# Router logits with stationary weights in four column groups, and the output norm's factors multiplied into the output weights

## The reference, cut to what matters

```python
o = jnp.concatenate([rms_norm(oa, p['out_norm_a']), rms_norm(ob, p['out_norm_b'])], axis=-1)
x = x + jnp.einsum('bse,ed->bsd', o, p['w_o'])
h2 = rms_norm(x, p['norm_ffn'])
x = x + expert_choice_moe(h2, p['w_router'], p['w_gate'], p['w_up'], p['w_down'])
...
logits = jnp.einsum('nd,de->ne', xf, w_router).astype(jnp.float32)
aff = jax.nn.softmax(logits, axis=-1)
gates, idx = lax.top_k(aff.T, cap)
```

## Time and profile before

| | |
|---|---|
| median of 3 runs | 1052.97 us (1052.86 to 1053.31) |
| the profiled execution | 1052.84 us |
| its span from the first to the last instruction | 1051.1 us |
| PE / DVE / ACT / POOL busy | 1015.7 / 897.5 / 780.7 / 504.9 us |
| mean granted TensorE clock | 0.992 |

### The profile page before, as it was taken

How to read it: one execution, slowest core, us unless ns; L and a number is a source line. 1 busy time by engine, 2 the same in 40 slices (tenths; PEclk the granted TensorE clock), 3 DMA queues, 4 the chain that set the end, 5 groups by cost and what they waited for, 6 DMA issues and landing times.

```text
span 1051.1 us, 16370 instructions
## 1 busy us (share of the span) xinstructions
PE 1015.7 (97%) x5361; PEld 865.1 (82%) x5361; DVE 897.5 (85%) x1128; ACT 780.7 (74%) x1071; POOL 504.9 (48%) x458
## 2 busy tenths in 40 slices
PE   8999999999999999995999999999999999999997
PEld 7999977888788888884888888888888888888885
DVE  6788779999988954478999999999999999999982
ACT  7665569999999844446778877788778877788772
POOL 2477689555599764544532444234432444234001
PEclk9999999999999999997999999999999999999999
DMA  9345150211332278753899999999999999999982
GB/s 324 80 127 121 69 203 16 47 32 41 111 95 78 85 212 261 207 171 121 346 377 398 405 413 401 401 398 420 399 403 399 400 418 401 402 397 415 408 343 40
DMA packets 83359, 272.90 MB, mean 260 GB/s; under 512 B 32929, under 2 KB 41340, under 8 KB 59500
## 3 DMA queue, kind: packets, MB, share of 16 engines
q1 hardware_dynamic: 77504, 254.96, 64.2%
q0 software_dynamic: 5744, 17.29, 6.6%
q10 hardware_dynamic: 60, 0.01, 0.0%
HBM read 245.89 MB, written 26.35 MB: 259 GB/s over the span
## 4 chain that ended last, share of the span: by engine, by line
PE 50%; DMA 1%; DVE 1%; issue 0%; ACT 0%; POOLq 0%; POOL 0%
PE ps L2166 11%; PE ps L2168 11%; PE ps L2167 11%; PE ps L2182 5%; PE ps L2181 5%; PE ps L2180 5%; PE ps L2133 1%; DMA out<-y,give 1%; DMA xt<-h,idxT 0%; DVE idx L1914 0%; DVE affT L1923 0%; DVE gates L1909 0%; POOLq L2440 0%; POOL out L2125 0%; ACT y L2294 0%
## 5 line engine op out<-in xcount | busy, mean ns | idle before, releaser
L2336 DVE TENSOR_TENSOR lo<-raw,hi 128x2048 fp32r<-128x2048 f32 x191 | 430.7, 2286 | 29.5 <-ACT hi L2258 29.3
L2258 ACT ACTIVATE hi<-raw 128x2048 fp32r<-128x2048 f32 x192 | 364.2, 1917 | 67.4 <-PE ps L2168 56.6
L2166 PE MATMUL ps<-hi,xehi 128*128 128x512 f32 x480 | 188.4, 393 | 0.1
L2168 PE MATMUL ps<-hi,xelo 128*128 128x512 f32 x480 | 187.1, 390 | 0.0
L2167 PE MATMUL ps<-lo,xehi 128*128 128x512 f32 x480 | 186.7, 389 | 0.0
L2090 POOL DMA_INDIRECT xe<-h,take x60 | 110.8, 1847 | 25.1 <-issue 13.7
L2085 POOL COPY take<-idx 128x4 uint32 (+1 forms) x15 | 31.0, 2066 | 188.6 <-DVE xt L2352 188.4
L2168 PEld LDWEIGHTS ps<-hi,xelo 128*128 128x128 f32 x480 | 90.1, 188 | 19.0
L2166 PEld LDWEIGHTS ps<-hi,xehi 128*128 128x128 f32 x480 | 90.3, 188 | 18.7 <-issue 0.5
L2167 PEld LDWEIGHTS ps<-lo,xehi 128*128 128x128 f32 x480 | 90.2, 188 | 18.4
L1445 DVE TENSOR_TENSOR probTlo<-ps,probThi 128x512 fp32r<-128x512 f32 x128 | 87.6, 684 | 14.9 <-ACT probThi L1400 12.4
(11 more groups left out here) (311 smaller groups left out, 2188.8 us busy)
## 6 DMA issues: line engine op xcount, KB each, us to landing
raw<-in_w_down SPq DMA_DIRECT2D x64, 1024.0 KB, 10.0
raw<-in_w_gate SPq DMA_DIRECT2D x60, 1024.0 KB, 10.0
raw<-in_w_up SPq DMA_DIRECT2D x60, 1024.0 KB, 9.6
w_raw<-in_w_in SPq DMA_DIRECT2D x8, 592.0 KB, 9.3
x<-in_x SPq DMA_DIRECT2D x8, 512.0 KB, 5.4
r<-reciprocal_sums SPq DMA_DIRECT2D x32, 128.0 KB, 3.1
attention_out<-pj SPq DMA_DIRECT2D x16, 256.0 KB, 2.5
woraw<-in_w_o SPq DMA_DIRECT2D x4, 1024.0 KB, 5.4
```

The lines of the kernel that those rows point to most:

```text
L2166: pe.matmul(ps[:, dst[n], :], rowhi[:, c, :], hi[w][:, cols], start=c == 0, stop=False)
L2168: last = pe.matmul(ps[:, dst[n], :], rowlo[:, c, :], hi[w][:, cols], start=False, stop=c == KD - 1)
L2258: act.activation(hi[s][:], raw[r][:], ACT.Copy).then_inc(hi_done, 1)
L2336: dve.tensor_tensor(lo[s][:], raw[r][:], hi[s][:].bitcast(F32), ALU.subtract).then_inc(lo_done, 1)
```

## The change

Two things are changed.

**The output norm's factors.** GpSimd multiplies each block of `w_o` (`woraw`, 128x1024) with its 128 factors, in place, ahead of the rounding: one tensor_scalar more for each of the eight blocks, with a wait for it. VectorE's `apply_gain` goes, and what read `gained` reads `o`. The load of `o` for tile `j`, which waited for `apply_gain` of tile `j - 2`, waits for its `otlo`.

**The router's logits.** For all tiles but the last, the router's weights are the stationary operand, padded to 32 columns (`wrwide`), and `h2T` is the moving one (128 columns). Chunk `c` writes the PSUM partitions from 32 * (c % 4), so that chunks 0 to 3 go to four groups of 32 columns of the array, and 4 to 7 are accumulated on them. ScalarE copies the 128x128 result to `parts`, and one more product with `picks`, which has four 16-wide pieces of the identity one above the other, adds up the four groups and gives 128x16 as before. The last tile's logits are made as before. GpSimd makes `wrwide` and `picks`.

```diff
@@ split_output_weights (attend, GpSimd)
             pool.wait_ge(wo_loaded, 16 * (2 if i < 4 else i // 2 + 1))
+            pool.tensor_scalar(raw, raw, k["gcol"][:, G_OUT + i:G_OUT + i + 1], None, ALU.mult).then_inc(wo_hi, 1)
+            pool.wait_ge(wo_hi, 2 * i + 1)
             pool.tensor_copy(wo["hi"][:, i, :], raw).then_inc(wo_hi, 1)
-            pool.wait_ge(wo_hi, i + 1)
+            pool.wait_ge(wo_hi, 2 * i + 2)
             pool.tensor_tensor(wo["lo"][:, i, :], raw, wo["hi"][:, i, :].bitcast(F32), ALU.subtract).then_inc(wo_lo, 1)
@@ vector_program (attend)
-            if u == NU - 3:
-                apply_gain(0, 0)
-            elif u == NU - 1:
+            if u == NU - 1:
                 o_low(0, 0)
-            elif u == NU:
-                apply_gain(0, 1)
             elif u == NU + 2:
                 o_low(0, 1)
@@ load_rows (route, SyncE)
-            sp.wait_ge(o_ready, 2 * (j - 1))
+            sp.wait_ge(otlo_done, 2 * (j - 1))
@@ gpsimd_pieces (route), rest
-            pool.tensor_tensor(wr[:], wr[:], k["gcol"][:, G_FFN:G_FFN + KD].unsqueeze(2).to_broadcast([P, KD, EXPERTS]),
+            pool.memset(wrwide[:, :, EXPERTS:32], 0.0).then_inc(wr_scaled, 1)
+            pool.tensor_tensor(wrwide[:, :, 0:EXPERTS], wr[:], k["gcol"][:, G_FFN:G_FFN + KD].unsqueeze(2).to_broadcast([P, KD, EXPERTS]),
                                ALU.mult).then_inc(wr_scaled, 1)
+            for a in range(GROUPS):
+                rows = slice(32 * a, 32 * a + 32)
+                pool.wait_ge(wr_scaled, 2 + a)
+                pool.tensor_copy(picks[rows, :], k["ident"][rows, 32 * a:32 * a + EXPERTS]).then_inc(wr_scaled, 1)
@@ tensor_pieces (route)
-        def logits(j):
+        def logit_parts(j):
...
             for c in range(KD):
-                if j == LAST and c == 0:
+                if c % GROUPS == 0:
+                    pe.wait_ge(x1t_copied, 2 * j + c // GROUPS + 1)
+                group = 32 * (c % GROUPS)
+                last = pe.matmul(PARTS[group:group + 32, :], wrwide[:, c, :], xT[:, c, :], start=c < GROUPS, stop=c >= GROUPS)
+            last.then_inc(logits_made, 1)
+
+        def logit_sums(j):
+            pe.wait_ge(logits_read, parts_made(j))
+            pe.matmul(LG, parts[:], picks[:], start=True, stop=True).then_inc(logits_made, 1)
...
                     at = 2 if j == LAST - 1 else 3
                     if j and c == at:
-                        logits(j - 1)
-                    if j and c == at + 1 and closes(j - 1):
+                        logit_parts(j - 1)
+                    if j and c == at + 1:
+                        logit_sums(j - 1)
+                    if j and c == (at + 2 if j == LAST - 1 else at + 3) and closes(j - 1):
                         pair_transposes(j - 1)
-            last_product(0, range(GROUP_CHUNKS, KD))
+            last_product(0, range(GROUP_CHUNKS, GROUP_CHUNKS + 1))
+            logit_sums(LAST - 1)
+            last_product(0, range(GROUP_CHUNKS + 1, KD))
@@ scalar_pieces (route)
+        def copy_parts(j):
+            act.wait_ge(logits_made, parts_made(j))
+            if j:
+                act.wait_ge(logits_made, made(j - 1))
+            act.activation(parts[:], PARTS, ACT.Copy).then_inc(logits_read, 1)
...
                 if j:
+                    copy_parts(j - 1)
                     exponentials(j - 1)
@@ vector_pieces (route), rest; the same at the other tiles
-                apply_gain(j + 1, 0)
-                apply_gain(j + 1, 1)
```

More of the change, by code:

```diff
@@ L270, in build @@
         wo["aff"] = [om(f"aff{i}", [P, 64]) for i in range(2)]
+        wo["wrwide"] = om("wrwide", [P, KD, 32])
+        wo["parts"] = om("parts", [P, P])
+        wo["picks"] = om("picks", [P, EXPERTS])
         assert om.at <= end
@@ L1408, in scalar_program, with vector_program @@
         route_rest()
-    def vector_program(dve, row_stats, query_stats, key_stats, rb_done, rk_done, apply_gain, o_low, route_rest):
+    def vector_program(dve, row_stats, query_stats, key_stats, rb_done, rk_done, o_low, route_rest):
         def prepare(kind, g):
@@ L1511, in route @@
     LAST = T - 1
-    o, gained, xr, h2, gffn, sq, wr, small, aff = (wo[n] for n in ("o", "gained", "x", "h2", "gffn", "sq", "wr", "small", "aff"))
+    o, xr, h2, gffn, sq, wr, small, aff = (wo[n] for n in ("o", "x", "h2", "gffn", "sq", "wr", "small", "aff"))
     osq, acc = wo["osq"], wo["acc"]
+    wrwide, parts, picks = wo["wrwide"], wo["parts"], wo["picks"]
     othi, otlo, x1, xT = (wo[n] for n in ("othi", "otlo", "x1", "h2T"))
@@ L1705, in logits, with last_logits @@
             else:
-                pe.wait_ge(wr_scaled, 1)
+                pe.wait_ge(wr_scaled, 2 + GROUPS)
             for c in range(KD):
-                if j == LAST and c == 0:
+                if c % GROUPS == 0:
[6 more added lines that the diff above has]
+            pe.matmul(LG, parts[:], picks[:], start=True, stop=True).then_inc(logits_made, 1)
+        def last_logits():
+            pe.wait_ge(logits_read, made(LAST - 1))
+            if PAIRS_DONE[LAST - 1]:
+                pe.wait_ge(at_done, PAIRS_DONE[LAST - 1])
+            for c in range(KD):
+                if c == 0:
                     pe.wait_ge(x1t_half, 1)
-                elif j == LAST and c == 4:
+                elif c == 4:
                     pe.wait_ge(x1t_copied, 2 * LAST + 1)
-                elif c % 4 == 0:
-                    pe.wait_ge(x1t_copied, 2 * j + c // 4 + 1)
-                last = pe.matmul(LG, xT[:, c, :], wr[:, c, :], start=(c == 0), stop=(c == KD - 1))
-            last.then_inc(lg_ready, 1)
+                last = pe.matmul(LG, xT[:, c, :], wrwide[:, c, 0:EXPERTS], start=(c == 0), stop=(c == KD - 1))
+            last.then_inc(logits_made, 1)
         def pair_transposes(j):
@@ L1745, in rest @@
             x_transposes(LAST, 1)
-            logits(LAST)
+            last_logits()
             pair_transposes(LAST)
@@ L1793, in exponentials @@
                 act.wait_ge(at_ready, ORDER[j] % TS - 1)
-            act.activation(pair[:, cols], LG, ACT.Exp, bias=nbias(j), scale=r2(j), accum_out=lsum(j)).then_inc(lexp_done, 1)
+            act.activation(pair[:, cols], LG, ACT.Exp, bias=nbias(j), scale=r2(j), accum_out=lsum(j)).then_inc(logits_read, 1)
         def scale_rows(j):
@@ L1840, in o_low @@
             dve.wait_ge(othi_done, 2 * j + b + 1)
-            dve.tensor_tensor(otlo[j % 2][:, cols, :], gained[min(j, 1)][:, cols, :], othi[j % 2][:, cols, :].bitcast(F32),
+            dve.tensor_tensor(otlo[j % 2][:, cols, :], o[j % 2][:, cols, :], othi[j % 2][:, cols, :].bitcast(F32),
                               ALU.subtract).then_inc(otlo_done, 1)
@@ L1964, in rest @@
             add_second(LAST - 2)
-            apply_gain(LAST, 0)
-            apply_gain(LAST, 1)
             group_means(LAST - 1)
@@ L1996, in rest @@
             merge()
-        return apply_gain, o_low, rest
+        return o_low, rest
     route_signals = {"merged": merged, "x1_stored": x1_stored, "h2_stored": h2_stored, "h2_done": h2_done}
```

36 lines of the change are left out of this document (15 added, 21 removed).

## The result

| | before | after |
|---|---|---|
| median of 4 runs each, in turn on one chip | 1053.14 us (1052.86 to 1054.13) | 1073.43 us (1071.18 to 1074.11) |
| ratio, 95% interval | | 1.0189 (1.0177 to 1.0201) |
| the profiled execution | 1052.84 us | 1074.11 us |
| its span | 1051.1 us | 1072.3 us |
| PE / DVE / ACT / POOL busy | 1015.7 / 897.5 / 780.7 / 504.9 us | 1018.9 / 883.1 / 782.6 / 526.5 us |

The changed kernel is slower, as forecast, but by 20.3 us and not by 5.7: above the range (1054.6 to 1064.0) and above every rival, the dearest of which was 1065.3.

The account below looks back on a forecast made before the run. TensorE was taken as the bound, except GpSimd from 276.70 us for 38 us and VectorE from 461.99; 5.6 (GpSimd) - 0.6 (VectorE) + 0.7 (tiles) = +5.7 us on 1052.84 gave 1058.5, range 1054.6 to 1064.0.

Parts of the forecast that it names:

- The multiplication on GpSimd: Output weights in attention: five multiplications at 1.12 us each ahead of step 24's rotary keys start head 25's scores 5.6 us later.
- the multiplication costs 2.39 us: Rival, GpSimd's output weights: priced as with two tensors, 12.4 us in place of 5.6, time 1065.3; chance 0.12.
- no delay: Rival at TensorE's wait at 315.65: GpSimd's time doesn't reach TensorE, 1052.9 us; chance 0.12.
- side by side: Rival, router's logits: four column groups work fully side by side, parts take 0.43 us, time 1055.0; chance 0.15.
- The last three multiplications cost nothing: Behind head 25: GpSimd 3.4 us later, values and copies still in time, o landing near 360.9, read at 362.91.
- The clock: Rival in attention: clock falls in new waits near 296 and 315, time 1061; chance 0.04.
- The multiplications taken from VectorE: End of attention: without apply_gain at 366.66, TensorE's wait for probTlo at 368.09 goes, -0.57 us.
- The logits: Router's tiles: parts take p = 1.0 us for 1.70, the ninth product costs 0.30, a tile saves 0.40 us.
- all follow one another: Rival, router's logits: no two records side by side, parts take 1.70 us, time 1063.4; chance 0.12.
- The wait that takes its place: Tiles two to six: TensorE waits for acc ahead of the squares, 0.42 us on average, losing 0.1 over five tiles.
- The seventh tile: From chunk 2's end to the pair's transposition: p - 0.03 longer, VectorE gets its affinities 1.0 us later.
- The last tile: VectorE's gap of 0.49 us at 479.67 shrinks since TensorE is 0.40 us quicker relative to it: -0.4 us.

Follow-up runs that it names:

- e6: e1 with GpSimd's tensor_scalar multiplying by the constant 1.0 instead of a factor per partition, factors left out: 1074.24 us, ratio 1.0198.
- e5: e1 with GpSimd copying each block of the output weights onto itself instead of multiplying it, factors left out: 1059.62 us, ratio 1.0061.
- e9: e5 with 24 transpositions that nothing reads on TensorE ahead of its wait at head 25: 1057.76 us, ratio 1.0044.
- e1: The kernel before with only the factors multiplied into the output weights on GpSimd, logits as they were: 1074.5 us, ratio 1.0201.
- e7: e1 with the factor given as a second tensor, one column broadcast over the row, to a tensor_tensor: 1067.01 us, ratio 1.0129.
- e8: e1 with the last three blocks of the output weights not multiplied, their factors left out: 1068.85 us, ratio 1.0150.
- e11: e2 with ScalarE's squares of the next tile made earlier and VectorE's second first-tile multiplication one step later: 1048.85 us, ratio 0.9960.
- e4: e2 with all eight chunks of the logit parts sent to one group of 32 columns: 1060.92 us.
- e10: e2 with 14 transpositions that nothing reads on TensorE in the last tile ahead of its wait for x1: 1051.00 us, ratio 0.9978.
- e2: The kernel before with only the logits in four column groups, factors still multiplied on VectorE: 1051.93 us, ratio 0.9985.

## Why the prediction was wrong, step by step

**What bounds the kernel** held. GpSimd from 276.5 us on, then its rotary keys, was the path, and what was lost ahead of the tiles reached the end one to one.

**The multiplication on GpSimd** is the step that failed, by its price. The mechanism and the place were right: five stand ahead of step 24 and five times the price comes out at head 25. The price was 2.85 + 0.08 and not 1.04 + 0.08: 14.4 us in place of 5.6. The argument was that a factor per partition is no second tensor, so that the row with one tensor is the nearest. The trace of before had no one-tensor arithmetic of this size on GpSimd, only a rounding. e6 shows that the kind of instruction is dear, and not its factor. The upper end, 2.39, was no bound either: it was the dearer of the two rows that I looked at, chosen by the number of tensors read, while the same trace had GpSimd's multiplication of 128x1024 at 3.04 us (line 1639). With that row as the end, head 25 would have been up to 5 x 3.12 = 15.6 us late. The rival *the multiplication costs 2.39 us* named the cause, and fell short of its size for this and the next two reasons. The range, too, left out more than it said: no delay, half of side by side and half of the dear multiplication are 0.12 + 0.075 + 0.06, 0.255 and not 0.2.

**"The last three multiplications cost nothing"** held for the price that it was made with (e5) and not for the real one. The cover was GpSimd's 5.4 us of idle time behind head 25; at 8.8 us it is gone, and GpSimd is late again for `ot`, for `o` and for the first `acc`. The prediction gave the cover's end as the load of `o`, and that came true: issued at 380.12, it lands 3.6 us later, at 383.7, when ScalarE has stood for 2.78 us. What releases it is not the split of the eighth block, though, as I had it: in the trace of before that ends at 344.62, and the load is issued at 353.95, behind the store of a pair of heads (351.61) that GpSimd scales last. The chain is GpSimd's all the same. The load was issued 26.2 us later than before: eight times 2.93 are 23.4, GpSimd waits 1.9 us more for TensorE at 334.38, and from the store to the load it is 3.36 us in place of 2.34. In e5 it was issued 9.7 us later, where the prediction makes 5.6 + 3.4 = 9.0, and it landed 2.4 us ahead of ScalarE's reading (369.81), where the prediction has 2.0.

**The clock** was given 0.04, as a rival that adds to the forecast by itself. It was there every time GpSimd's keys were late and nothing filled the wait: 1.6 us behind a wait of 3.00 (e5; e9 takes it away), 1.6 to 2.35 behind waits of 4.70 to 6.68 (the first two units of head 25: 5.26 us in e1, 5.73 in e7, 5.79 in e8, 5.99 in the changed kernel, 3.64 before), and 2.96 in e6 (6.60 us). The price of the rival, half of some 5 us, was about right. A clock below 1.00 ahead of 480 us was among the prediction's own signs of being wrong. The row on which I put it aside, waits below 1 us that left it at 1.00, says nothing of a wait of 3 to 7 us, and that there would be such a wait followed from the forecast itself.

**The multiplications taken from VectorE**: -0.57 was predicted, -0.95 measured (e5). The instruction named is worth 0.6 when it alone is moved (e11). In e5 it is 0.48 of the 0.95, and the other 0.47 lie one step earlier: TensorE's wait for the `probTlo` ahead of it, 1.05 us before (366.89), is 0.57 in e5. There VectorE's `otlo` stands in front, and it starts at the same distance from TensorE's values in both, but takes 0.99 us in e5 and 1.47 before. Why it is shorter no run tells; VectorE has two multiplications less there, and reads `o` in place of `gained`.

**The logits.** p = 1.0 was predicted, 0.67 measured. My picture, that only the second record of a product lies beside the first of the next, is wrong: e4 gives 1.86 us where nothing lies side by side, and 0.57 is nearer to a fourth of that, 0.47, than to half. The end for "all follow one another", 1.70, was 0.25 too low (1.86 and the 0.09 ahead of it). The ninth product costs 0.24 (0.13 and 0.11 behind it), not 0.30. So a tile saves 1.70 - 0.67 - 0.24 = 0.79, twice the 0.40 of the sum.

**The wait that takes its place** was there, and its sum over five tiles, 2.1, is what the prediction had: five times 0.79 less the 1.86 measured. But it was made by four tiles of five: in one the chain was just quick enough. The sizes of the waits in the rows, 0.23 to 0.33, are about half of what each costs.

**The seventh tile**: p - 0.03 gives 0.64 with the measured p; measured 0.59. **The last tile**: -0.4 was predicted, +0.75 measured. The relation of the engines was right, as e10 shows (16.38 against 16.76, -0.38). What was missed is that TensorE, further ahead of VectorE by what the logits save and by the later pair, waits 1.89 us for `x1` in place of 0.55, and loses its clock.

**Added up**, the error of 15.6 us (21.3 measured in the profiled executions against 5.7) is: price of five multiplications 8.8; what was left uncovered and the clock behind head 25, 7.1 (6.1 and the 0.95 that hides in it); the first `acc` 1.3; the last tile's clock 1.2; against these the tiles -2.0 and small ones of -0.8.

## What to carry to other kernels

An instruction that the trace doesn't show at its size is bounded by no row that merely looks like it: GpSimd took 1.04, 1.89, 2.39, 2.85 and 3.04 us for different instructions on 128x1024, and the count of tensors doesn't order them. Look first for the same operation anywhere in the trace, in another part of the kernel or at another size: here a multiplication stood in it, far from the place of the change, and nearer to the price than both rows used. Ask of each "costs nothing" up to which price it holds, and of each new wait on TensorE what the clock does behind it; the two together made more than half of the error. Work that is taken from an engine with room and put on one that bounds a stretch loses even at the small price (e5, 6.2 us for eight copies); the other half of this change, which moved work to idle parts of the same array, won.

## What was unexpected of the hardware

- On GpSimd, 128x1024 in place: a copy 1.04 us, a product with a repeated column as a second tensor 1.89, with a constant 2.78, with a factor per partition 2.85, of two full tensors 3.04. A subtraction of two tensors into a third, rounded, 2.39.
- Sixteen records with 32 stationary and 128 moving columns: 0.57 us in four column groups, 1.86 in one. The entry into 32 columns costs 0.09 us in both.
- The granted clock fell to its lower level (0.50, that is 1.2 GHz) behind all waits of TensorE of 2.68 us and more, in attention and in the tiles (up to 6.68), and stayed at 1.00 behind all of 1.83 and less. (The wait of 1.36 ahead of the last transposition of the affinities, with little work on TensorE around it, is left out: the microsecond behind it has 0.50 in e1 and 1.00 in e10.) Between them the length doesn't decide: it fell behind 1.89 (changed kernel, `x1`), 1.90 (e2), 2.03 and 2.56 (e7) and 2.19 (e1), and stayed behind 1.91 (changed kernel, 305.75), 1.96 (e8), 2.07 and 2.65 (e6) and 2.50 (e1). No run here tells what does. On the critical path the lower clock cost between 0.9 and 2.96 us each time.
- Transpositions that nothing reads, put into such a wait, made the kernel 1.9 us (e9) and 0.9 us (e10) faster.
